# Attention stage: output weights split in quarters over the steps, the last values and turns in other PSUM banks, compressed turns at two steps

## What is computed

```python
def nsa_layer(h, norm_g, w_in, gate_b, q_norm_g, w_out, k_cmp, v_cmp, k_s, v_s, k_w, v_w):
    ...
    o = lax.map(nsa_single, (q, gates, k_cmp, v_cmp, k_s, v_s, k_w, v_w))
    return o.reshape(B, S, N_HEADS * HEAD_DIM) @ w_out

def nsa_single(args):
    ...
        o = gt[:, 0][..., None] * o_cmp + gt[:, 1][..., None] * o_slc + gt[:, 2][..., None] * o_win
```

## Time and profile before

| what | value |
|---|---|
| median of 3 runs | 2362.54 us (2361.96 to 2364.03) |
| the profiled execution | 2363.0 us, span 2361.4 us |
| PE busy | 2308.6 us, 98% |
| DVE busy | 1698.5 us, 72% |
| ACT busy | 1376.8 us, 58% |
| PE in the chain that ended last | 94% of the span |
| mean granted clock of PE | 0.993 of full speed |
| the stage that the diff touches | about 397 to 475 us |

### The profile page before, as it was taken

The page is one execution under the profiler, slowest core; times in us unless marked ns, Lnnn a source line. Parts: engine busy times, 40 slices in busy tenths (PEclk is TensorE's granted clock), DMA queues, the critical chain, the costliest instruction groups (busy, mean ns, idle before and its releaser), DMA issues.

```text
span 2361.4 us, 31652 instructions
## 1 busy us (share of the span) xinstructions
PE 2308.6 (98%) x12274; PEld 1946.2 (82%) x12274; DVE 1698.5 (72%) x1612; ACT 1376.8 (58%) x1253; POOL 100.3 (4%) x111
## 2 busy tenths in 40 slices
PE   7999999999999999999999989999999999999998
PEld 6978857888889978888899788888888888888886
DVE  6655555655556776455666668888888898989897
ACT  4633314553446855433567457777777777777775
POOL 0000020000001100000011001000000000000020
PEclk9999999899999999999999999999999999999999
DMA  6555345155435336455243389999999999999992
GB/s 219 184 209 213 143 138 191 51 214 213 175 115 182 109 108 248 162 195 213 94 166 108 138 319 414 393 387 371 380 377 391 368 391 368 390 368 384 375 387 120
DMA packets 204633, 588.63 MB, mean 249 GB/s; under 512 B 9164, under 2 KB 17552, under 8 KB 204544
## 3 DMA queue, kind: packets, MB, share of 16 engines
q1 hardware_dynamic: 197696, 564.28, 64.3%
q0 software_dynamic: 6656, 23.04, 2.6%
q10 hardware_dynamic: 192, 0.05, 0.0%
HBM read 573.19 MB, written 14.16 MB: 249 GB/s over the span
## 4 chain that ended last, share of the span: by engine, by line
PE 94%; DVE 3%; ACT 1%; issue 1%; DMA 1%; ACTq 0%; DVEq 0%
PE ps L1406 9%; PE ps L1405 9%; PE ps L1407 9%; PE ps L782 8%; PE ps L784 8%; PE ps L783 8%; PE ps L1445 4%; PE ps L1444 4%; PE ps L1446 4%; PE ps L667 4%; PE ps L677 3%; PE ps L676 3%; PE ps L678 3%; PE ps L659 2%; PE ps L1179 1%; PE ps L1180 1%
## 5 line engine op out<-in xcount | busy, mean ns | idle before, releaser
L2072 DVE TENSOR_TENSOR more_low<-more_parts,high_parts 128x2048 fp32r<-128x2048 f32 x192 | 432.0, 2288 | 35.3 <-ACT high_parts L1514 34.3
L1514 ACT ACTIVATE high_parts<-more_parts 128x2048 fp32r<-128x2048 f32 x192 | 364.5, 1918 | 101.3 <-PE ps L1446 51.8
L1405 PE MATMUL ps<-high_parts,xmh 128*128 128x512 f32 x896 | 352.8, 394 | 2.4 <-issue 2.4
L1407 PE MATMUL ps<-high_parts,xml 128*128 128x512 f32 x896 | 349.4, 390 | 0.0
L2072 DVE TENSOR_TENSOR raw_low<-raw,high_parts 128x2048 fp32r<-128x2048 f32 x144 | 324.1, 2288 | 27.8 <-ACT high_parts L1514 27.8
L1514 ACT ACTIVATE high_parts<-raw 128x2048 fp32r<-128x2048 f32 x144 | 275.8, 1920 | 93.2 <-PE ps L1407 49.8
L1641 ACT ACTIVATE wh<-raw 128x4096 fp32r<-128x4096 f32 (+1 forms) x57 | 196.8, 3452 | 190.0 <-PE ps L784 176.8
L2250 DVE TENSOR_TENSOR wl<-raw,wh 128x4096 fp32r<-128x4096 f32 (+1 forms) x57 | 239.3, 4197 | 71.7 <-ACT wh L1641 71.7
L782 PE MATMUL ps<-wh,xh 128*128 128x512 f32 (+1 forms) x632 | 244.2, 386 | 3.1 <-issue 2.5
L784 PE MATMUL ps<-wh,xl 128*128 128x512 f32 (+1 forms) x632 | 239.9, 380 | 0.0
L783 PE MATMUL ps<-wl,xh 128*128 128x512 f32 (+1 forms) x632 | 239.7, 379 | 0.0
(11 more groups left out here) (555 smaller groups left out, 4464.7 us busy)
## 6 DMA issues: line engine op xcount, KB each, us to landing
more_parts<-in_moe_w_gate SPq DMA_DIRECT2D x78, 1024.0 KB, 5.3
more_parts<-in_moe_w_up SPq DMA_DIRECT2D x66, 1024.0 KB, 7.2
raw<-in_moe_w_down SPq DMA_DIRECT2D x64, 1024.0 KB, 6.3
more_parts<-in_moe_w_down SPq DMA_DIRECT2D x48, 1024.0 KB, 6.7
raw<-in_moe_w_up SPq DMA_DIRECT2D x46, 1024.0 KB, 5.3
raw<-in_w_in SPq DMA_DIRECT2D x22, 2048.0 KB, 8.1
raw<-in_f_w_in SPq DMA_DIRECT2D x20, 2048.0 KB, 8.5
raw<-in_moe_w_gate SPq DMA_DIRECT2D x34, 1024.0 KB, 6.7
```

What stands on the lines that cost most here:

```text
L1405: mm(o, xmh[:, k, :], hi[:, cs], start=(k == 0), stop=False)
L1407: t = mm(o, xml[:, k, :], hi[:, cs], start=False, stop=(k == KD - 1))
L1514: fn(part_high(j), part_raw(j), ACT.Copy).then_inc(hi_done, 1)
L2072: v.tensor_tensor(part_low(j), part_raw(j), part_high(j).bitcast(F32), ALU.subtract).then_inc(lo_done, 1)
```

## The change

Five edits, all in the attention stage:

- The rounding of output-weight parts q = 0 and 1 is cut into quarters of 128x512. ACT does those of q = 0 at i = 2 to 5 and of q = 1 at i = 6 to 9; DVE does the rests at i = 6 to 9 and 10 to 13. Only the last quarter of a part signals.
- The compressed tile `m` = 0 is turned and copied at i = 1, `m` = 1 at i = 2.
- The values of steps 14 and 15 go to banks 7 and 6, the banks of the scores of step 14, instead of both to bank 2.
- The last two turned outputs go to banks 5 and 1 instead of both to bank 5.
- PE does the first `out_begin` before the last two turns instead of between them.

```diff
-                self.w = Ring([2], w_filled, w_read)
+                self.w, self.w_last = Ring([2], w_filled, w_read), Ring([7, 6], w_filled, w_read)
...
+                self.on_last = Ring([5, 1], on_filled, on_read)
...
+        COMPRESSED_AT = [1, 2]
+
+        HIGH_STEP, LOW_STEP = [2, 6], [6, 10]
+        LAST_VALUES = len(STEPS) - 2
...
-                b = me.w.claim(pe)
+                if i == LAST_VALUES:
+                    me.w_last.n = me.w.n
+                b = (me.w if i < LAST_VALUES else me.w_last).claim(pe)
...
-                b = me.on.claim(pe)
+                b = (me.on_last if j else me.on).claim(pe)
...
-                if i == 1:
-                    me.see(pc_ready)
-                    for m in range(M):
-                        b = me.pc.claim(pe)
...
+                if i in COMPRESSED_AT:
+                    m = COMPRESSED_AT.index(i)
+                    if m == 0:
+                        me.see(pc_ready)
+                    b = me.pc.claim(pe)
...
-            turn_outputs(1, 1)
+            drained(me.on)
+            me.on_last.n = me.on.n
             me.see(mh_ready)
             me.see(ml_ready)
             drained(me.pt)
             b = me.g.claim(pe)
             out_begin(1, b, (0,))
+            turn_outputs(1, 1)
             turn_outputs(0, 1)
             out_begin(1, b, (1,))
-            drained(me.on)
+            drained(me.on_last)
...
-                if i in (4, 6):
-                    high_out(1, i // 2 - 2)
+                for q in range(2):
+                    if 0 <= i - HIGH_STEP[q] < 4:
+                        if i == HIGH_STEP[q]:
+                            arrived(act, out_key(1, q))
+                        ks = slice(2 * (i - HIGH_STEP[q]), 2 * (i - HIGH_STEP[q]) + 2)
+                        t = fn(wmo[:, q, ks], out_view(1, q)[:, ks], ACT.Copy)
+                        if i == HIGH_STEP[q] + 3:
+                            t.then_inc(mh_ready, 1)
...
-                if i in (5, 7):
-                    low_out(1, (i - 5) // 2)
+                for q in range(2):
+                    if 0 <= i - LOW_STEP[q] < 4:
+                        if i == LOW_STEP[q]:
+                            me.see(mh_ready)
+                        ks = slice(2 * (i - LOW_STEP[q]), 2 * (i - LOW_STEP[q]) + 2)
+                        t = v.tensor_tensor(out_view(1, q, raw_low)[:, ks], out_view(1, q)[:, ks], wmo[:, q, ks].bitcast(F32),
+                                            ALU.subtract)
+                        if i == LOW_STEP[q] + 3:
+                            t.then_inc(ml_ready, 1)
```

More of the change, by code:

```diff
@@ L1101, in _ @@
                     values(i - 1)
-                if i == 1:
-                    me.see(pc_ready)
-                    for m in range(M):
-                        b = me.pc.claim(pe)
-                        for g in range(NG):
-                            t = tr(ps[:, b, g * P:(g + 1) * P], pcp[:, m, g * HPG:(g + 1) * HPG, :].rearrange("p h c -> p (h c)"), ident)
-                        t.then_inc(pc_filled, 1)
+                if i in COMPRESSED_AT:
[3 more added lines that the diff above has]
+                    b = me.pc.claim(pe)
+                    for g in range(NG):
+                        t = tr(ps[:, b, g * P:(g + 1) * P], pcp[:, m, g * HPG:(g + 1) * HPG, :].rearrange("p h c -> p (h c)"), ident)
+                    t.then_inc(pc_filled, 1)
                 if i in TURN_AT:
@@ L1799, in high_outputs @@
             def high_outputs(m, j):
-                b = me.on.take(act)
+                b = (me.on_last if j else me.on).take(act)
                 fn(uh[:, 4 * j:4 * j + 4, m * P:(m + 1) * P], ps[:, b, :].rearrange("p (k t) -> p k t", k=4), ACT.Copy).then_inc(on_high, 1)
@@ L1807, in _ @@
                     probs(i + 1)
[L1808 to L1811, removed]
+                if i in COMPRESSED_AT:
+                    m = COMPRESSED_AT.index(i)
+                    b = me.pc.take(act)
+                    fn(pcT[:, m].rearrange("p g t -> p (g t)"), ps[:, b, :], ACT.Copy).then_inc(pc_read, 1)
                 if i in TURN_AT:
                     high_outputs(*TURN_AT[i])
-                if i in (4, 6):
-                    high_out(1, i // 2 - 2)
+                for q in range(2):
[6 more added lines that the diff above has]
+                            t.then_inc(mh_ready, 1)
+            me.on_last.n = me.on.n
             act.wait_ge(zero_sent, 16)
@@ L2489, in outputs @@
                 st_ = stat[:, i % 3, :]
-                b = me.w.take(dve)
+                if i == LAST_VALUES:
+                    me.w_last.n = me.w.n
+                b = (me.w if i < LAST_VALUES else me.w_last).take(dve)
                 o = ps[:, b, 0:4 * (HD + 1)].rearrange("p (a w d) -> p a w d", a=2, w=2)
@@ L2503, in low_outputs @@
             def low_outputs(m, j):
-                b = me.on.take(dve)
+                b = (me.on_last if j else me.on).take(dve)
                 me.see(on_high)
```

## The result

| | before | changed |
|---|---|---|
| median | 2361.96 us (2358.75 to 2364.03, 5 runs) | 2349.49 us (2347.59 to 2353.03, 5 runs) |
| profiled execution | 2363.0 us, span 2361.4 | 2353.0 us, span 2351.4 |
| ratio | | 0.9949, interval 0.9938 to 0.9961 |

The changed kernel is 12.5 us faster by the medians. The forecast was 2354.0 us with a range of 2350.7 to 2359.0: right in sign, 1.2 us outside the range, and too small in size. Measured again, beside the last experiments, the changed kernel took 2351.08 us (2347.62 to 2354.61, 6 runs) against 2360.44 us before, ratio 0.9959 (0.9947 to 0.9971). That is just inside the range, so the spread of runs decides on which side of it one measurement falls; the size is 9 to 12 us where 8.5 were forecast.

A forecast was written before the change was run, and what follows sets the result against it. The prediction took PE (98% busy) to bound the kernel, with only its waits and low-clock time to win back. Middle 6.1, compressed turn 1.0, end 4.0, less 2.6 for the clock, made 8.5 us: 2354.0 us, range 2350.7 to 2359.0.

The forecast's parts named there:

- the clock at the end: End of the attention stage: the clock falls once more, about the values of step 14 or 15, costing 2.6 us.
- The lengths of the end at full clock: Last scores to the projection needing all outputs: pieces summed to 14.5 us instead of 18.50, gain 4.0 us.
- the best case: The whole kernel without a clock fall at the end: all 11.1 us back, 2351.4 us.
- The middle: Steps 7 to 10, around the split: 6.3 us excess less 0.2 us, so 6.1 us back.
- undisturbed pairs: Steps 7 to 10: two pairs of 6.46 us and one 1.9 us turn of outputs make 14.8 us.
- DVE's shortage: Steps with quarters on DVE: DVE is 0.29 us short in each pair; PE loses 0.2 us in the middle.
- The compressed turn: Start of the stage: two compressed tiles turned in separate steps take 0.9 us instead of 1.88, gain 1.0 us.
- The end: Last scores to the projection needing all outputs: 4.0 us gained at full clock, less 2.6 us for a clock fall.
- DVE's lateness: At i = 13 DVE is some 0.5 us late, which falls on the maxima of step 15; charged to the end.
- No fall at the end: Rival, end of the stage: the clock stays up, all 11.1 us come back, 2351.4 us; chance 0.25.
- only waits come back: Rival, whole stage: the clock falls as before whatever the small waits do; 2.8 us back, 2359.7 us; chance 0.11.
- The slower rival: Rival, steps 6 to 8 and 11 to 13: DVE's shortage makes PE wait at half clock; 2373.4 us; chance 0.04.

The follow-up runs named there:

- e6: The changed kernel with DVE's split whole again (at i = 6 and 10), ACT's in quarters: 2354.08 us, ratio 0.997 to the kernel before.
- e10: The changed kernel with ACT's weight copies whole again (at i = 4 and 6), DVE's in quarters: 2349.38 us, ratio 0.9948 to the kernel before.
- e1: The kernel before with the quarters alone, on both engines; banks, order at the end and compressed turns as before: 2356.13 us, ratio 0.9977.
- e4: The changed kernel with the end as before (values in bank 2, turns in bank 5, old order): 2355.75 us, ratio 0.9973 to the kernel before.
- e7: The changed kernel with the values of steps 14 and 15 in bank 2 again: 2356.95 us, ratio 0.9986 to the kernel before.
- e2: The kernel before with the edits at the end alone (banks of last values and turns, projection order): 2356.06 us, ratio 0.9975.
- e3: The changed kernel with both whole splits of before: 2356.01 us, ratio 0.9969 to the kernel before.
- e8: The changed kernel with the last two turns in bank 5 and the old order at the end: 2352.28 us, ratio 0.9963 to the kernel before.
- e12: The changed kernel with the edit of e9, run again beside the changed kernel: 2349.53 us, ratio 0.9951 to the kernel before.
- e9: The changed kernel with 6 of 12 projection matmuls moved into the wait for the exponentials of step 15: 2350.38 us, ratio 0.9959 to the kernel before.
- e5: The kernel before with 6 extra matmuls, results never read, in PE's waits at i = 7 and again at i = 9: 2359.88 us, ratio 0.9999.

## Why the prediction was wrong in size

The step that failed is the clock at the end: the prediction charged 2.6 us for one more fall, and there was none. The lengths of the end at full clock were too large by 1.0 us besides. The other terms held. In the medians, 4.5 us lie between forecast and measurement: 3.7 of them in the stage (3.6 at the end, 0.1 in the rest), 0.6 because the kernel before came out at 2361.96 us beside the changed one and not at 2362.54, and 0.2 within the spread of runs. The low end of the range, 2350.7 us, allowed 0.7 us for the spread of runs below the best case and nothing for an error in the sizes.

**The middle** (forecast 6.1 us back, measured 6.34): right. The sum by undisturbed pairs held: 14.83 us against my 14.8. DVE's side of the split is the cause: whole on DVE it costs PE 1.24 us each time (e6), whole on ACT nothing (e10). How much of the 6.34 us is clock differs between executions: with whole splits the middle took 19.6, 19.7 and 21.2 us. I allowed 0.2 us for DVE's shortage; it cost 0.07 us, and in the piece behind (14.83 us in e1, e4 and e7, 14.76 in e2 and e3).

**The compressed turn** (1.0 forecast, 0.91 measured): right; the tile at 407.17 takes 0.54 us to the next start, where I counted 0.43 to 0.45.

**The end** (1.4 forecast, 5.02 measured): wrong, in two steps.

- *The clock at the end.* I charged 2.6 us for a fall after the wait for the last exponentials, as "nearer to the two cases that fell". The wait came as told (0.50 us, with 0.97 us for the 4 transposes) and the clock stayed up. It stayed up at the end of all nine profiles with the values in two banks: the changed kernel, e2, e3, e6, e8 to e12; in seven of them the wait was there (0.41 to 0.50 us), in e9 and e12 it was filled. It fell in all five with one bank: before, e1, e4, e5, e7. What differs ahead of the fall is the wait of 0.22 to 0.30 us for DVE's outputs behind the transposes. In four of the five the low clock set in before the long gap of 1.6 us was reached (before: by 462 us, the gap from 464.96 - 1.59 = 463.37); in e5 it set in inside the gap. I saw the short wait and priced it at 0.23 us. The Trainium skill, "TensorE: Matmul & The Clock Gate", section "HAM oscillation — how this bites in real kernels", lays a fall to a long wait for data. The runs disagree here: in four of five the clock fell before the longest wait came. The two waits that went away with the second bank had thus cost 6.8 to 10.2 us of low clock in each of these five, and taking them away was what kept the clock; the wait that stayed didn't lower it.
- *The length at full clock.* 13.48 us against my 14.5. The transposes of step 15 are done 454.91 - 450.75 = 4.16 us after the scores, not 4.7: the wait for the exponentials grew from 0.41 to 0.50 us, so DVE's lateness cost 0.1 us and not 0.5. The values of steps 14 and 15 take 457.51 - 454.91 = 2.60 us, not 2.80. The two turns take 462.50 - 459.02 = 3.48 us and the matmuls around them 1.51 + 1.73, together 6.72 us and not 7.0: a turn is 1.74 us, where I counted 1.9.

So of the 3.6 us by which the end came out better, 2.6 are the clock and 1.0 the sizes.

**The rivals.** "No fall at the end", with a chance of 0.25, was the right case in kind, and its 11.1 us is 1.1 us short by the sizes. That only waits come back doesn't fit the profiles: 12.2 us came back in the stage, of which the waits removed are 0.69 + 0.59 + 0.30 + 0.23 + 1.59 = 3.4 us; half of the low 10 us of the earlier trace rows is 5.0, half of the 4.91 us that PE was busy in the other low stretch 2.5, and the other 1.3 lie in the stretched transposes and turns around the waits. The slower rival was wrong: DVE runs without idle time in steps 6 to 8 and 11 to 13, as the prediction said, and PE doesn't wait for it.

**Not settled.** Which of two equal pairs of waits lowers the clock (e3: the second, e2: the first), and how long it stays low (3.4 to 10.2 us), differs between executions. The changed kernel and the version with the filled wait have two profiles each, every other kernel has one, so how often the clock falls at a place isn't known; for the end, the mean clocks of the runs (e7) say that with one bank it falls in most. Waits are not all that lowers the clock, as the fall at 386 us shows; what else does wasn't tried. Whether the wait of 0.3 us by itself decides at the end wasn't tried apart from the gap of 1.6 us, with which it comes; only the order in time speaks for it. Why the filler's gain is missing in the total is open, beyond what the mean clocks show in e5.

## What to carry to other kernels

Where one engine is 98% busy, look for the stretches in which its clock is halved and list the waits just ahead of them. Two short waits close together, 0.60 + 0.30 us, cost 3.2 us with the half clock behind them once (e3), and 1.7 us without it the other time. One PSUM bank too few for the last two results cost 4.7 us in the stage, of which 1.9 us were waits (e7); a second bank, taken from buffers that just came free, removed both. Matmuls with no open inputs can be moved into a wait: that gave back 0.6 us (e9), and in one profile dummy matmuls kept the clock up, without a gain in the total (e5). Cut a long side task only on the engine that others wait for (DVE, 1.24 us each time); on the other the quarters brought nothing.

## What was unexpected in the hardware

- The clock can be low with PE busy throughout: from 428 to 438 us in the kernel before PE was busy 10.00 of 10 us at 0.50, from 386 to 393 us in the changed one 7.00 of 7 us at 0.51. So a low stretch isn't found by looking for idle time. Nor need there be any ahead of it: PE was busy 10.00 of 10 us before the fall at 386 us, at last with matmuls of 128x30.
- Low stretches of 3.4 to 10 us come and go elsewhere in the program between executions of the same or nearly the same code; runs of the kernel before ranged from 2357.4 to 2366.6 us on one chip. A difference of a few us must be read in the stage, not in one total, and the stage in more than one profile where the clock takes part.
- A DVE subtraction of 128x512 from SBUF takes 0.68 us but its follower starts after 0.60, so four take 2.4 us of DVE against 2.2 for the whole.
